# Fox and band attention on one Trainium2 core: which engine copies the turned probabilities, and where ScalarE's exponentials stand

## What is computed

```python
def attend(q, k, v, bias, valid):
    s = jnp.einsum('bqhd,bkhd->bhqk', q, k).astype(jnp.float32) * SCALE + bias
    s = jnp.where(valid, s, -jnp.inf)
    p = jax.nn.softmax(s, axis=-1)
    return jnp.einsum('bhqk,bkhd->bqhd', p.astype(v.dtype), v)

def trunk_layer(x, ...):
    h = rmsnorm(x, norm_mix_pre)
    qa, ka, va, logf, qb, kb, vb = project_in(h, w_in, b_forget)
    oa = fox_fn(qa, ka, va, logf)
    ob = band_fn(qb, kb, vb)
    ...
    mix = jnp.concatenate([oa, ob], axis=-1) @ w_out
    x = x + rmsnorm(mix, norm_mix_post)
    hf = rmsnorm(x, norm_ffn_pre)
    ff = (jax.nn.silu(hf @ w_gate) * (hf @ w_up)) @ w_down
    return x + rmsnorm(ff, norm_ffn_post), ...
```

## Time and profile before

| | |
|---|---|
| median of 3 runs | 3207.45 us |
| the profiled execution | 3205.57 us, span 3203.8 us |
| TensorE matmul / weight load busy | 2921.2 us (91%) / 2618.4 us (82%) |
| VectorE / ScalarE busy | 1661.8 us (52%) / 1209.6 us (38%) |
| granted TensorE clock, mean | 0.97 |

### The profile page before, as it was taken

The page is one execution under the profiler, slowest core; times in us unless marked ns, Lnnn a source line. Parts: engine busy times, 40 slices in busy tenths (PEclk is TensorE's granted clock), DMA queues, the critical chain, the costliest instruction groups (busy, mean ns, idle before and its releaser), DMA issues. The chain is left out here.

```text
span 3203.8 us, 57072 instructions
## 1 busy us (share of the span) xinstructions
PE 2921.2 (91%) x23073; PEld 2618.4 (82%) x23073; DVE 1661.8 (52%) x3253; ACT 1209.6 (38%) x2124; POOL 471.6 (15%) x402
## 2 busy tenths in 40 slices
PE   7999999798888778869958999999999987998998
PEld 7999999677777556648848999999999985886887
DVE  6222212276667556744437766786676644224444
ACT  5330000166667456644424334333433323123221
POOL 0000000100000000001114533453433420000000
PEclk9999999899999899989988999999999998999999
DMA  5321221322211776445542333333233225435553
GB/s 168 90 80 65 74 72 61 110 78 78 72 38 57 238 249 197 147 141 152 165 149 105 106 107 107 127 107 107 89 107 106 91 87 163 105 94 151 166 171 120
DMA packets 275868, 376.37 MB, mean 117 GB/s; under 512 B 16456, under 2 KB 203864, under 8 KB 263576
## 3 DMA queue, kind: packets, MB, share of 16 engines
q1 hardware_dynamic: 273368, 368.43, 36.2%
q10 hardware_dynamic: 2240, 4.30, 0.4%
HBM read 283.52 MB, written 89.15 MB: 116 GB/s over the span
## 5 line engine op out<-in xcount | busy, mean ns | idle before, releaser
L2091 PE MATMUL dwn_py<-dwn_wh,dwn_ah 128*128 128x512 f32 x748 | 297.0, 397 | 42.3 <-DVE dwn_al L2166 32.7
L1143 ACT ACTIVATE att_pts<-att_pt 128x384 f32<-128x384 f32 (+3 forms) x444 | 208.4, 494 | 246.6 <-PE att_pt L1027 229.7
L2092 PE MATMUL dwn_py<-dwn_wl,dwn_ah 128*128 128x512 f32 x748 | 294.5, 394 | 0.0
L2093 PE MATMUL dwn_py<-dwn_wh,dwn_al 128*128 128x512 f32 x748 | 294.1, 393 | 0.0
L1027 PE MATMUL att_pt<-att_eye,att_sx 64*128 64x64 f32 x3296 | 177.6, 235 | 103.1 <-ACT att_pts L1143 67.2
L1132 ACT ACTIVATE att_sx<-att_sx,att_nm 128x640 f32<-128x640 f32 (+17 forms) x272 | 265.0, 975 | 10.6 <-DVE att_nm L1260 10.6
L1027 PEld LDWEIGHTS att_pt<-att_eye,att_sx 64*128 64x128 f32 x3296 | 131.2, 140 | 167.0 <-ACT att_pts L1143 98.8
L79 PE MATMUL frt_pz<-frt_xhi,frt_hi 128*128 128x448 f32 (+1 forms) x640 | 230.5, 360 | 0.0
L81 PE MATMUL frt_pz<-frt_xhi,frt_lo 128*128 128x448 f32 (+1 forms) x640 | 230.5, 360 | 0.0
L80 PE MATMUL frt_pz<-frt_xlo,frt_hi 128*128 128x448 f32 (+1 forms) x640 | 230.0, 359 | 0.0
L1063 PE MATMUL att_po<-att_pts,att_vv 128*64 128x128 f32 x3296 | 214.0, 278 | 0.0
(11 more groups left out here) (251 smaller groups left out, 7465.8 us busy)
## 6 DMA issues: line engine op xcount, KB each, us to landing
gup_wr<-in_w_gu SPq DMA_DIRECT2D x65, 1024.0 KB, 5.2
dwn_ar<-mid_act SPq DMA_DIRECT2D x67, 704.0 KB, 6.2
att_raw<-out_zT SPq DMA_DIRECT2D x64, 256.0 KB, 3.4
att_bb<-in_cache_ak SPq DMA_DIRECT2D x16, 1024.0 KB, 9.0
att_bb<-in_cache_av SPq DMA_DIRECT2D x16, 1024.0 KB, 9.6
mid_act<-gup_ao SPq DMA_DIRECT2D x44, 362.0 KB, 2.4
out_zT<-frt_shared SPq DMA_DIRECT2D x64, 224.0 KB, 1.9
frt_raw<-in_w_slab SPq DMA_DIRECT2D x11, 1024.0 KB, 5.3
```

The costliest lines, as they stand in the source:

```text
L1143: nc.scalar.activation(pts[G % NPT][:, :, 0:k, 64 * x:64 * x + 64], pt[x][:].rearrange("p (e j q) -> p e j q", e=2, q=64)[:, :, 0:k, :], A ...
L2091: nc.tensor.matmul(out, ah[u][:, j, :], wh[:, j, :], start=(j == 0), stop=False)
L2092: nc.tensor.matmul(out, ah[u][:, j, :], wl[:, j, :], start=False, stop=False)
L2093: last = nc.tensor.matmul(out, al[u][:, j, :], wh[:, j, :], start=False, stop=(j == NJ - 1))
```

## The change

Three things, all in `attend`. First, `LONG[G]` says whether a long gap follows turn G. VectorE copies `pt[1]` where the gap is short (120 turns), and ScalarE makes both copies where it is long. Second, ScalarE makes its copies of a turn before any exponential. Third, `exps_after(n)` puts the exponentials of job n + 1 behind the turns of job n that have a long gap behind them: one each behind the first two such turns, or both behind the same turn where the job has only one (in jobs of four and three turns that is behind turns 0 and 2, in jobs of two turns both behind turn 0).

```diff
+    TURNS = turn_list(ORDER)
+    LONG = [bool(VALUES[x]) for x in TURNS[1:]] + [True]
+    DVES = counted(0 if x else 1 for x in LONG)
+    LONGS = [[g for g in range(len(job_groups(n))) if LONG[T0[n] + g]] for n in range(NJOB)]
     def by_dve(G, x):
-        return x == 1 and G % 2 == 0
+        return x == 1 and not LONG[G]
     def copies(G, dve):
-        return (G // 2 + 1) if dve else 2 * (G + 1) - (G // 2 + 1)
+        return DVES[G + 1] if dve else 2 * (G + 1) - DVES[G + 1]
+    def exps_after(n):
+        if not LONGS[n]:
+            return 0, len(job_groups(n)) - 1
+        return LONGS[n][0], LONGS[n][1 if len(LONGS[n]) > 1 else 0]
...
                 def copied(G):
                     pe.wait_ge(s_ca, copies(G, False))
-                    pe.wait_ge(s_cd, copies(G, True))
+                    after(pe, s_cd, copies(G, True))
...
-                        copy(n, g, 0)
-                        if more and g == 0:
-                            exps(n + 1, 0)
-                        copy(n, g, 1)
-                        if more and g == (0 if last_of(n, 0) else 1):
-                            exps(n + 1, 1)
+                        for x in range(2):
+                            copy(n, g, x)
+                        for e in range(2):
+                            if more and g == exps_after(n)[e]:
+                                exps(n + 1, e)
```

More of the change, by code:

```diff
@@ L650, in value_order, with turn_list @@
     return out
+def turn_list(order):
+    return [(n, g) for what, n, g in order if what == "turn"]
 def attend(nc, t, keep, neg_c):
```

## The result

| | before | after |
|---|---|---|
| median | 3207.62 us | 3169.28 us (4 runs, 3164.17 to 3170.58) |
| ratio | | 0.9880, interval 0.9863 to 0.9898 |
| span of the profiled execution | 3203.8 us | 3168.1 us |
| attention, first to last job | 771.6 us | 732.6 us |

The kernel is 38 us faster. Forecast were 52 us, time 3154, range 3137 to 3178: the sign and the range hold, the sum is 14 us too good. It gives 39.0 us, all of the gain (the spans differ by 35.7 us, because attention's first job starts 2.6 us later in the second trace). The stages behind, from attention's end to the span's, take 1803.3 us before (3203.8 - 1400.5) and 1804.1 after (3168.1 - 1364.0): only moved, as forecast.

What follows compares the result with a forecast made beforehand. In attention TensorE, busiest, idled about 122 of 778 us, 100 of it waiting for ScalarE's copies and exponentials. Terms: 39 - 4 + 24.4 - 5 + 7.5 - 2 - 8 = 52 us, giving 3154 us, range 3137 to 3178.

Steps and rivals of the forecast that it cites:

- Part 1: In jobs of two turns, the second exponential moves from the short gap to turn 0's long gap; gain 39 us.
- rival (d): No change: copies and exponentials leaving the short gaps only uncover a wait behind them, for `att_nm` or `att_ot`; chance 0.04.
- Part 2: VectorE makes one of the two copies in 95 short gaps where ScalarE made both; gain 24.4 us after corrections.
- The 5 us taken off for a late VectorE: Short gaps: VectorE still busy at the turn's end in 28 of 120, partly also for shortened rounds; 5 us off.
- (a): VectorE's work in a round of attention becomes the bound; gain only 22 us, 3183 us; chance 0.14.
- (b): Slower: VectorE's copy in the 120 short gaps is late as a rule; 3227 us at 0.65 us lateness; chance 0.05.
- Part 3: In long gaps ScalarE makes both copies before any exponential; gain 7.5 us, mostly in three-turn jobs.
- for which 2 were taken: One-turn jobs and streams: exponentials come later behind the copy of `pt[1]`; between 0 and 6 us lost, 2 taken.
- for which 4 were taken: Behind the 8 two-turn streams two exponentials don't fit the long gap, the copy comes late; 8 x 0.5 = 4 us.
- Given back to DMA: Two DMA-bound stretches, ending at 1088 and 1186 us, where gains only lengthen a wait; 2 x 4 = 8 us lost.
- The likeliest case: The forecast itself: attention gains 38 to 65 us; chance 0.70.

Runs made afterwards that it cites:

- the pair without bursts: Kernels before and after, each with the next pair's values and bias loaded later and only a quarter of the streams' caches loaded: 3189.36 and 3138.34 us.
- the edit of the queries: VectorE's `block_queries` one job earlier, except the first stream's: 3162.39 us on the kernel after, 3202.46 us on the kernel before.
- the copies alone: Against the kernel before, only VectorE's copies moved to the short gaps, ScalarE's exponentials left where they stood: 3208.94 us, ratio 1.0006.

## Why the prediction was right, and where it was too good

**The mechanism is shown.** The earlier trace rows named the two waits. Both parts that were to shorten them do: the exponentials' wait falls to 6.6 us, and in band jobs a short gap of three tiles is 0.27 us shorter from the end of one turn to the start of the next (0.97 to 0.70 us).

**Part 1, the term that was mis-sized.** The prediction: "Gain: 56 x 0.69 = 39 us." The waits were worth that: from first load to middle, the first turns behind a job of two turns (59 by my count now) take 40.9 us less after the change than before, and a single wait 0.66. The wrong step is to take the wait removed for time gained. Put back by itself, Part 1 is worth 12.5 us by ratio and 10.6 in the jobs, for 34.5 us of waits.

In 12 of the places the saving, and the short gap's in the same jobs, only uncovered `block_queries`: TensorE's wait for it went from 2.6 to 13.8 us. These jobs save 7.9 us of waits and 1.9 in their short gaps, and their long gaps get 9.8 us longer. That is most of the 12.4 us that the pair without bursts lacks (60 - 47.6), and with the edit of the queries on both kernels the 12 jobs do gain 10 us: the 6 in front of the first 8 streams 5.6, the 6 others 4.1. The profile's page gave no hint, but the waits had the row of 2.6 us; its idle time was short because a longer wait stood just ahead of it. In rival (d), "only uncover a wait behind them", I had the mechanism, and dismissed it because all other waits together were 20 us. That sum tells how long these waits are now. It says nothing of how long they will be when the ones ahead of them go.

**Part 2.** The two gaps came out at the length forecast: three tiles above, four tiles here, 1.60 us by loads (the prediction: 1.59):

```profile
879.61 0.57 PEld L1041 LDWEIGHTS att_pt<-att_eye,att_sx 64*128 64x128 f32 x16 [0.17 <-issue]
...
880.42 0.68 DVE L1284 COPY att_pts<-att_pt 128x512 f32<-128x512 f32 x1
881.21 0.60 PEld L1041 LDWEIGHTS att_pt<-att_eye,att_sx 64*128 64x128 f32 x16 [0.63 <-ACT att_pts L1157]
```

The 5 us taken off for a late VectorE were about right: in the 120 short gaps its copy starts 0.04 us behind the turn's end in 84 and at most 0.42 us, but for one of 1.75 (the streams' constants, above). What goes beyond 0.04 comes to 5.6 us together. The 10.1 us in which turns wait for it, 0.6 us in each of 16 places, are mostly the normal length of a gap. Rivals (a) and (b) both needed it late as a rule, and are refuted. VectorE's copy is the longer one still (556 ns against 488 for 128x384, as in the earlier trace rows), which costs nothing side by side.

**Part 3** is as forecast. Turn 1 of a three-turn job, after the change:

```profile
870.83 0.87 ACT L1157 ACTIVATE att_pts<-att_pt 128x384 f32<-128x384 f32 x2 [0.40 <-PE att_pt L1041]
...
871.59 1.47 ACT L1146 ACTIVATE att_sx<-att_sx,att_nm 128x1408 f32<-128x1408 f32 x1
872.28 0.45 PEld L1041 LDWEIGHTS att_pt<-att_eye,att_sx 64*128 64x128 f32 x12 [0.17 <-issue]
```

0.17 us of idle loads in place of 1.09; the long gaps behind turn 0 of the three-turn jobs give 6.1 us, the forecast's number. Its price is small, as forecast: the 32 one-turn jobs of both kinds lose about 1 us together, for which 2 were taken. The two-turn streams, for which 4 were taken, lose 2.3 us. But the forecast had Part 3 as a small term of 7.5 us; it is also what lets Part 2 pay at all, as the copies alone show.

**Given back to DMA.** The prediction took 8 us, in two stretches. By the table it is 8.6 us (47.6 - 39.0). That the size agrees is in part luck, since the places were half right: the jobs 64 to 103, with both stretches in them, give back 3.6 us. One of the two stalls forecast:

```profile
1160.41 0.63 ACT L1133 ACTIVATE att_qh<-att_raw 128x512 fp32r<-128x512 f32 x1 [8.67 <-DMA att_raw<-out_zT]
...
1161.63 0.90 PE L1041 MATMUL att_pt<-att_eye,att_sx 64*128 64x64 f32 x12 [7.52 <-ACT att_pts L1157]
```

It is 8.67 us where the earlier trace rows had 8.2. Another 4 us, though, are lost in the 16 two-turn fox jobs (3.9 in place of 7.8 us), in front of which the 3 MB of values and bias are issued. I had looked for transfers that already stalled something; these had not, because the rounds were 1 us longer each.

**The range.** Part 1's 39 us lacked a term for what stands behind the waits, 10 us in the 12 jobs alone; no other term was off by more than a few us. The likeliest case had 38 to 65 us; 38.3 is its edge.

## What to carry to other kernels

A wait that is short in the trace may be short because a longer one stands ahead of it. Before pricing the removal of a wait times its count, follow the next instruction of the waiting engine in each *kind* of round, and ask when its input will be ready if the engine comes earlier; here 12 of the 71 two-turn jobs had an input that came almost as late already.
Where two engines share copies and one of them also has a long operation in its queue, who does which copy and what stands between the copies must be changed together: one alone gave nothing, and both 15 us on top of the other.
When rounds get shorter, look again at large loads that are issued ahead of small ones that an in-order engine waits for; moving 3 MB behind eight pieces of 256 KB was worth 14 us after the change and 9 before.

## What the runs showed of the hardware

The granted clock of TensorE can fall behind a short stop, and doesn't always. In the rows of windows above, the pair 2 job with 1.6 us of idle time is followed by one at 0.73, in which part of the time is at 1.2 GHz and the rest at 2.4, and 6.28 us of matmuls do what 5.03 us do at 1.00. The like stop of pair 1, 1.5 us of 5.83, is followed by a job at 1.00. Both of these next jobs take the same time (6.36 and 6.35 us). The two stalls of over 7 us have the lower clock too: this is the kernel after around the first of them.

```profile
1059.60:1071.30 11.70, 4.13 (x58) 3.65 (x60) 2.52 (x11) 3.03 (x7) 0.22 (x1) 0.77 0.96 312
```

What the lower clock costs behind a stall was not measured apart from the stall.
